# A gate's modulation product moved from TensorE to VectorE in a fused decoder layer

## The reference

```python
sc = jax.nn.silu(c)
mod = sc @ ada_w[l] + ada_b[l]                  # (1024) @ (1024 x 6144)
sh1, sc1, g1, sh2, sc2, g2 = jnp.split(mod, 6)
xn = rmsnorm(x, norm1_g) * (1.0 + sc1) + sh1
proj = xn @ w_in                                # q, k, v, ca, cg
...                                             # 8 heads of causal attention beside
...                                             # a gated convolution of width 31 with group norm
x = x + g1 * (y_mix @ w_out)
xn2 = rmsnorm(x, norm2_g) * (1.0 + sc2) + sh2
h = causal_dwconv(xn2 @ w_up, ffn_dw_w, ffn_dw_b)   # 1024 -> 2 x 2816, width 3
u, g = jnp.split(h, 2, axis=-1)
x = x + g2 * ((silu(g) * u) @ w_down)
```

## Time and profile before

| | |
|---|---|
| runs | 353.32, 354.15, 357.48 us |
| the profiled execution | 354.59 us; from its first to its last instruction (span) 352.8 us |
| mean granted TensorE clock | 0.995 |
| busy, share of the span | TensorE 96%, VectorE 68%, ScalarE 51%, GpSimd 24% |
| moved | 80.05 MB, 227 GB/s over the span |
| chain that ended last | TensorE 88%, DMA 3%, VectorE 3%, ScalarE 2% |

### The profile page before, as it was taken

One profiled execution on the slowest core, in us unless ns is written; L12 is line 12 of the kernel. 1 busy time (PEld: TensorE's weight loads), 2 busy tenths in 40 slices (PEclk: granted clock), 3 DMA queues, 4 the chain that ended last, 5 costly groups with the idle time before them and its releaser, 6 DMA issues.

```text
span 352.8 us, 6291 instructions
## 1 busy us (share of the span) xinstructions
PE 337.0 (96%) x2480; PEld 292.3 (83%) x2480; DVE 239.7 (68%) x467; ACT 178.8 (51%) x266; POOL 85.3 (24%) x134
## 2 busy tenths in 40 slices
PE   7789899999999989999999999999999999999995
PEld 6557788887565468999999999999999989898984
DVE  2654649999964664059886967675858585858556
ACT  4543763444126676547856636373636455454520
POOL 6372099729134086920000000000000000000000
PEclk9989999999999999999999999999999999999999
DMA  7999968989997995330755745554655555400003
GB/s 271 426 424 421 418 255 333 354 307 334 420 352 285 412 378 211 121 119 4 278 200 164 247 185 197 173 207 153 228 154 204 180 180 206 152 0 2 0 2 120
DMA packets 13090, 80.05 MB, mean 227 GB/s; under 512 B 1402, under 2 KB 2818, under 8 KB 3844
## 3 DMA queue, kind: packets, MB, share of 16 engines
q1 hardware_dynamic: 12852, 79.50, 59.5%
q10 hardware_dynamic: 144, 0.13, 0.1%
q0 software_dynamic: 64, 0.01, 0.0%
HBM read 78.57 MB, written 1.06 MB: 226 GB/s over the span
## 4 chain that ended last, share of the span: by engine, by line
PE 88%; DMA 3%; DVE 3%; ACT 2%; issue 2%; SPq 1%; POOL 0%; POOLq 0%; ACTq 0%
PE bank L962 25%; PE bank L964 24%; PE bank L963 24%; PE bank L984 4%; DMA raw<-in_stream 3%; PE bank L1015 2%; ACT w_hi L399 1%; PE bank L1228 1%; DVE prob L813 1%; PE bank L1029 1%; PE bank L1389 1%; PE bank L1345 1%; PE bank L1385 1%; PE bank L1132 1%; PE bank L1386 1%
## 5 line engine op out<-in xcount | busy, mean ns | idle before, releaser
L962 PE MATMUL bank<-act_hi,w_hi 128*128 128x256 f32 x528 | 152.1, 288 | 3.4 <-ACT act_hi L428 1.1
L963 PE MATMUL bank<-act_lo,w_hi 128*128 128x256 f32 x528 | 149.5, 283 | 0.0
L964 PE MATMUL bank<-act_hi,w_lo 128*128 128x256 f32 x528 | 149.5, 283 | 0.0
L962 PEld LDWEIGHTS bank<-act_hi,w_hi 128*128 128x128 f32 x528 | 101.3, 192 | 11.3 <-issue 8.4
L963 PEld LDWEIGHTS bank<-act_lo,w_hi 128*128 128x128 f32 x528 | 101.4, 192 | 0.5
L964 PEld LDWEIGHTS bank<-act_hi,w_lo 128*128 128x128 f32 x528 | 101.4, 192 | 0.0
L399 ACT ACTIVATE w_hi<-raw 128x2048 fp32r<-128x2048 f32 x45 | 85.9, 1908 | 19.7 <-DMA raw<-in_stream 13.7
L637 DVE TENSOR_TENSOR w_lo<-raw,w_hi 128x2048 fp32r<-128x2048 f32 x32 | 73.3, 2292 | 23.2 <-ACT w_hi L399 23.2
L361 POOL TENSOR_TENSOR w_lo<-raw,w_hi 128x256 fp32r<-128x256 f32 (+1 forms) x68 | 63.4, 967 | 38.0 <-ACT w_hi L399 26.5
L722 DVE SCALAR_TENSOR_TENSOR bank<-glu,cols,bank 128x256 f32<-128x256 f32 x116 | 46.0, 480 | 4.2 <-ACT bank L459 4.2
L387 POOL TENSOR_TENSOR xmod<-xr,qk 128x256 f32<-128x256 f32 x1 | 0.7, 722 | 195.7 <-DVE qk L951 195.7
(11 more groups left out here) (186 smaller groups left out, 337.5 us busy)
## 6 DMA issues: line engine op xcount, KB each, us to landing
raw<-in_stream SPq DMA_DIRECT2D x71, 1024.0 KB, 6.3
xt<-in_x_t SPq DMA_DIRECT2D x2, 512.0 KB, 4.6
bias<-toeplitz_rows SPq DMA_DIRECT2D x1, 1024.0 KB, 11.1
xt<-in_x_t SPq DMA_DIRECT2D x1, 1024.0 KB, 8.7
out<-xmod SPq DMA_DIRECT2D x3, 256.0 KB, 2.0
gate<-gate_rows SPq DMA_DIRECT2D x2, 256.0 KB, 6.0
gates_b<-in_ada_b_gates SPq DMA_DIRECT2D x1, 256.0 KB, 8.0
cols<-in_cols SPq DMA_DIRECT2D x1, 185.0 KB, 5.5
```

Of the source, the lines that this page charges most:

```text
L962: nc.tensor.matmul(o, sh, mh, start=first, stop=False)
L963: nc.tensor.matmul(o, sh, ml, start=False, stop=False)
L964: return nc.tensor.matmul(o, sl, mh, start=False, stop=last)
```

## The change

The DRAM image of the weights stays as it is; which halves of its slots are loaded together, and when, changes. Eight slots ("first_half", k) hold g1 and sh2 of row block k, four slots ("scale2", i) hold sc2 of two row blocks, four slots ("gate2", i) hold g2 of two row blocks. Each is loaded by two DMAs of 512 KB. The first twelve stand where the first twelve late ada slots stood; the four places behind them are gone, so the tiles from out 1 on stand four places earlier. The gate2 slots stand ahead of down 2 to down 5.

TensorE takes the twelve slots (`late_row`). g2 is summed by VectorE: eight products of silu(c)'s column with 128x1024 of a slot, added up in `g2_part` (`g2_products`), two behind each of down 1 to down 4. Two matmuls with ones then sum over the partitions ahead of down 6 (`g2_sum`), into bank `UP_BANK[0][0]`; VectorE adds the bias (`g2_rows_out`), and up 16 waits for that. The DMAs of g2's rows go from SP's queue to GpSimd's. g1 and sh2 are turned together, and VectorE reads both (`gate1_shift2_columns`).

```diff
@@ -50,12 +50,35 @@
+def loads():
+
+    late = [("first_half", k) for k in range(KT)] + [("scale2", i) for i in range(KT // 2)]
+    order = []
+    for kind, i in STREAM:
+        if kind == "ada" and i >= KT:
+            if late:
+                order.append(late.pop(0))
+            continue
+        if kind == "down" and 2 <= i < 2 + KT // 2:
+            order.append(("gate2", i - 2))
+        order.append((kind, i))
+    return order
+
+
+LOADS = loads()
+ROWS_USED = {x: n for n, x in enumerate(x for x in LOADS if x[0] in ("ada", "first_half", "scale2"))}
+ARRIVED = {x: 16 * sum(2 if y[0] in HALVES else 1 for y in LOADS[n % RAW:n + 1:RAW]) for x, n in AT.items()}
+G2_SUM_AT = 6
...
-            for n, (kind, i) in enumerate(STREAM):
+            for n, (kind, i) in enumerate(LOADS):
                 if n >= RAW:
-                    k0, i0 = STREAM[n - RAW]
+                    if k0 == "gate2":
+                        sp.wait_ge(g2_step, 2 * i0 + 2)
+                    elif (k0, i0) in ROWS_USED:
+                        sp.wait_ge(ada_used, ROWS_USED[k0, i0] + 1)
                     else:
                         low_made(sp, SP_AT[k0, i0])
-                sp.dma_start(raw[:, n % RAW, :], stream[n]).then_inc(raw_ready[n % RAW], 16)
+                if kind == "first_half":
+                    halves = [(FROM["ada", KT + i], 0), (FROM["ada", 2 * KT + i], 0)]
+                elif kind == "scale2":
+                    halves = [(FROM["ada", 2 * KT + 2 * i + h], 1) for h in range(2)]
+                elif kind == "gate2":
...
+                for to, (row, half) in enumerate(halves):
+                    sp.dma_start(raw[:, n % RAW, to * D_MODEL:(to + 1) * D_MODEL],
+                                 stream[row, :, half * D_MODEL:(half + 1) * D_MODEL]).then_inc(raw_ready[n % RAW], 16)
...
-                if (kind, i) == ("out", 2):
-                    sp.wait_ge(mod_rows_ready, 1)
-                    sp.dma_start(gate_rows, gates_b[64:97:32, :]).then_inc(gates_stored, 16)
...
-                if (kind, i) == ("up", 3):
-                    sp.wait_ge(gates_stored, 16)
-                    sp.wait_ge(qk_ssq, 1)
-                    for n in range(2):
-                        sp.dma_start(gate[:, 0, n * 512:n * 512 + 512], bass.AP(gate_rows.tensor, 512 * n, [[0, P], [1, 512]])
-                                     ).then_inc(gate2_ready, 16)
@@ -382,6 +412,14 @@
+            pool.wait_ge(g2_rows, 1)
+            pool.dma_start(gate_rows, gates_b[64:97:32, :]).then_inc(gates_stored, 16)
+            pool.wait_ge(gates_stored, 16)
+            pool.wait_ge(qk_ssq, 1)
+            for n in range(2):
+                pool.dma_start(gate[:, 0, n * 512:n * 512 + 512], bass.AP(gate_rows.tensor, 512 * n, [[0, P], [1, 512]])
+                               ).then_inc(gate2_ready, 16)
+
...
-            def g1_out():
-
-                act.wait_ge(gates_turned, 1)
-                nc.scalar.activation(g1[:, :].rearrange("p (q j) -> p q j", q=2),
-                                     bank[2][:, :].rearrange("p (j q r) -> p q j r", j=4, q=4)[:, 0:2, :, 0],
-                                     ACT.Copy).then_inc(g1_ready, 1)
+            def sh2_rows_out():
+
+                act.wait_ge(ada_used, 2 * KT)
+                act.wait_ge(glu_ready, CT)
+                nc.scalar.activation(gate_rows1[64:, :], bank[2][64:, :], ACT.Copy).then_inc(sh2_rows, 1)
...
             split_hi(SP_AT["out", 0])
+            sh2_rows_out()
             gn_rows()
...
-                if p == 0:
-                    g1_out()
-                elif p == 1:
+                if p == 1:
                     mod_rows_out()
                     split_hi(SP_AT["out", 1])
                 elif p == 2:
...
+            def gate1_shift2_columns():
+
+                dve.wait_ge(gates_turned, 1)
+                turned_rows = bank[2][:, :].rearrange("p (j q r) -> p q j r", j=4, q=4)
+                nc.vector.tensor_copy(g1[:, :].rearrange("p (q j) -> p q j", q=2), turned_rows[:, 0:2, :, 0]).then_inc(g1_ready, 1)
+                nc.vector.tensor_tensor(shift[:, 1, :].rearrange("p (q j) -> p q j", q=2), turned_rows[:, 2:4, :, 0],
+                                        cols_of("sh2_b").rearrange("p (q j) -> p q j", q=2), ALU.add).then_inc(mod_cols_read, 1)
+
...
+                turned_rows = bank[TURN_BANK][:, :].rearrange("p (j q r) -> p q j r", j=4, q=4)
+                scale2 = scale[:, 1, :].rearrange("p (q j) -> p q j", q=2)
+                nc.vector.tensor_tensor(scale2, turned_rows[:, 0:2, :, 0], cols_of("sc2_b").rearrange("p (q j) -> p q j", q=2),
+                                        ALU.add).then_inc(mod_cols_read, 1)
+                dve.wait_ge(mod_cols_read, 2)
+                nc.vector.tensor_tensor(scale2, turned_rows[:, 2:4, :, 0], scale2, ALU.add).then_inc(mod_cols_read, 1)
+                dve.wait_ge(mod_cols_read, 3)
                 nc.vector.scalar_tensor_tensor(scale[:, 1, :], scale[:, 1, :], 1.0, cols_of("norm2_g"), ALU.add,
                                                ALU.mult).then_inc(mod_cols_read, 1)
-                dve.wait_ge(mod_cols_read, 2)
+                dve.wait_ge(mod_cols_read, 4)
...
+            def g2_products(i):
+
+                arrived(dve, "gate2", i)
+                for h in range(2):
+                    k = 2 * i + h
+                    some = slot("gate2", i)[:, h * D_MODEL:(h + 1) * D_MODEL]
+                    if k == 0:
+                        dve.wait_ge(silu_c_ready, 1)
+                        nc.vector.tensor_scalar(g2_part, some, silu_c[:, k:k + 1], None, ALU.mult).then_inc(g2_step, 1)
+                    else:
+                        dve.wait_ge(g2_step, k)
+                        nc.vector.scalar_tensor_tensor(g2_part, some, silu_c[:, k:k + 1], g2_part, ALU.mult,
+                                                       ALU.add).then_inc(g2_step, 1)
+
+            def g2_rows_out():
+
+                dve.wait_ge(g2_summed, 1)
+                nc.vector.tensor_tensor(gates_b[64:, :], bank[UP_BANK[0][0]][64:, :], gates_b[64:, :], ALU.add).then_inc(g2_rows, 1)
...
-            dve.wait_ge(ada_used, 2 * KT)
-            dve.wait_ge(gates_b_ready, 16)
-            nc.vector.tensor_tensor(gates_b[:, :], bank[2][:, :], gates_b[:, :], ALU.add).then_inc(mod_rows_ready, 1)
+            g1_rows()
...
                 if p == 0:
+                    gate1_shift2_columns()
                     gn_scale()
...
-            norm2_columns()
+            scale2_columns()
@@ -929,7 +998,11 @@
                 done = m > m0 and SPLIT[m - 1][0] == "up"
                 if done:
                     earlier_taps(SPLIT[m - 1][1])
+                if m > m0 and SPLIT[m - 1] == ("down", G2_SUM_AT):
+                    g2_rows_out()
                 split_lo(m + 2)
+                if m > m0 and SPLIT[m - 1][0] == "down" and 1 <= SPLIT[m - 1][1] <= KT // 2:
+                    g2_products(SPLIT[m - 1][1] - 1)
                 if done:
                     gate_hidden(SPLIT[m - 1][1])
                     hid_low(SPLIT[m - 1][1])
...
+            def late_row(kind, i):
+
+                arrived(pe, kind, i)
+                to = bank[2] if kind == "first_half" else bank[7]
+                if (kind, i) == ("scale2", 0):
                     pe.wait_ge(tap, PAIR_TAPS[0])
                 for q in range(4):
-                    last = nc.tensor.matmul(bank[to][32 * q:32 * q + 32, :], silu_c[:, k:k + 1].to_broadcast([P, 32]),
-                                            slot("ada", n)[:, 512 * q:512 * q + 512], start=(k == 0), stop=(k == KT - 1))
+                    k = i if kind == "first_half" else 2 * i + q // 2
+                    last = nc.tensor.matmul(to[32 * q:32 * q + 32, :], silu_c[:, k:k + 1].to_broadcast([P, 32]),
+                                            slot(kind, i)[:, 512 * q:512 * q + 512], start=(i == 0),
+                                            stop=(i == (KT if kind == "first_half" else KT // 2) - 1))
                 last.then_inc(ada_used, 1)
...
             pair_scores(0)
             late_ada(1)
             gn_turn()
-            late_ada(1)
             head_turn(0)
             turn_gates()
             head_turn(1)
@@ -1301,13 +1369,12 @@
             pair_scores(1)
             pe.wait_ge(v_ready, ST)
             pair_values(0)
-            late_ada(2)
             head_turn(2)
-            late_ada(1)
             head_turn(3)
             pair_scores(2)
             pair_values(1)
             pe.wait_ge(g1_ready, 1)
+            pe.wait_ge(mod_cols_read, 1)
             pe.wait_ge(gn_scaled, CT)
...
+                if t == 2 * G2_SUM_AT + 4:
+                    pe.wait_ge(g2_rows, 1)
...
+            def g2_sum():
+
+                pe.wait_ge(g2_step, KT)
+                pe.wait_ge(tap0, 2 * (2 * G2_SUM_AT + 3))
+                for q in range(2):
+                    last = nc.tensor.matmul(bank[UP_BANK[0][0]][64 + 32 * q:96 + 32 * q, :], ones[:, 0:32],
```

(5 more changed lines are left out.)

58 lines of the change are left out of this document (28 added, 30 removed).

## The result

The changed kernel takes 360.58 us, the median of 3 runs (357.26 to 361.80), against 354.15: 1.0154 times the kernel before, 95% interval 1.0096 to 1.0212. A second set of six runs gave 360.88 us and 1.0151 (1.0091 to 1.0211). The forecast was 355.5 us, its range ended at 357.6. The profiled execution took 361.8 us, its span is 360.0 us, its mean granted clock 0.972 (before 0.995).

What follows compares the result with a forecast made beforehand. TensorE was taken as the bound, busy 337.0 of 352.8 us. Profiled 354.59 - 0.4 (removal) + 1.8 (sum's wait) = 356.0, put at 355.5 us because the median lies 0.44 below the profiled run; range 353.2 to 357.6 us.

Steps and rivals of the forecast that it cites:

- Rival (b): Attention stage: with slots removed TensorE's clock falls to half, costing about 1.7 us, ending at 357.1 us; chance 0.20.
- the later places: Removed slots, two behind pair 0's values, one between heads 2 and 3: at most 0.16 and 0.42 us gained, not adding.
- the first place: Removed slot behind the group norm's turning, at 110.48 us: worth 0, since head 0 starts at 112.16 us either way.
- The removal brings 0.4 us: Attention stage: four modulation slots leave TensorE, 3.8 us of work, of which 0.4 us comes off the end.
- The sum and its wait, 1.8 us: Ahead of up 16: TensorE waits for VectorE's bias addition, 1.8 us of delay, two matmuls inside it; ends 0.5 and 2.3.
- the 0.7 that was to show it: Sign near 292 us: a gap of 0.7 to 1.1 us on TensorE ahead of up 16, released by VectorE.
- The second norm: One more VectorE instruction for the second scale, covered by 6.67 us of idle time at 149.79 us: cost 0.
- The products: Among the down tiles: eight VectorE products of 128x1024, 1.22 us each (0.6 to 1.9), cost 0.
- The halved loads: Twelve slots arrive as two DMAs of 512 KB each; conv 3 is the tightest consumer: cost 0.
- (c): Rival: the half-slot loads land late, 1.7 us at conv 3, ending at 357.2 us; chance 0.05.
- (d): Rival: VectorE bounds the down tiles; products of 3.0 us lose 0.7 us in each of four rounds, 358.3 us; chance 0.03.
- The 0.97 for within 2%: Whole kernel: chance 0.97 that the time stays within 2% (7 us); slower 0.02, faster 0.01.

Runs made afterwards that it cites:

- e5: The changed kernel timed once more, nothing altered: 360.88 us, 1.0151 times the kernel before.
- e8: The changed kernel with 17 unused transposes at the start and VectorE's bias addition right behind the taps of up 15: 359.83 us, ratio 1.0117.
- e9: The kernel before with 17 unused transposes at the start, its last four modulation slots cut to one matmul of one column each: 355.04 us, ratio 1.0013.
- e13: The kernel before with 17 unused transposes at the start, its last four modulation slots wholly off TensorE, ring places freed early: 357.68 us, ratio 1.0051.
- e14: e8 with one matmul of one column at each of the four places of the removed slots: 357.99 us, ratio 1.0103.
- e7: The kernel before with 17 unused transposes on TensorE at the start: 354.17 us, ratio 0.9974.
- e11: e8 with an unused stand-in for the removed slot ahead of head 0 only: 359.25 us, ratio 1.0077.
- e10: e8 with three unused stand-ins behind pair 0's values and between heads 2 and 3: 356.53 us, ratio 1.0036.
- e12: e7 with seven more unused transposes around the second norm: 353.65 us, 0.9951 times the kernel before.
- e2: The changed kernel with an unused stand-in for only the removed slot between the group norm's turn and head 0: 357.97 us, ratio 1.0098.
- e3: The changed kernel with three unused stand-ins behind pair 0's values and between heads 2 and 3, none ahead of head 0: 356.73 us, ratio 1.0070.
- e6: The kernel before with three of the four matmuls left out in each of the last four modulation slots: 354.70 us, ratio 0.9996.
- e4: The changed kernel with all four removed slots replaced by unused stand-ins and VectorE's bias addition right behind the taps of up 15: 356.87 us, ratio 1.0075.
- e1: The changed kernel with unused stand-in matmuls at all four places of the removed slots: 359.50 us, ratio 1.0104.

## Why the prediction was wrong

**The clock is the step that failed.** Rival (b) described the mechanism and its place, had a chance of 0.20 and a price of one fall of 3.4 us at half its length, 1.7 us (the sum behind it wrote 1.6). Emptying the places brought a fall in the profiled run and, over e5, e8, e9, e13 and e14, 7.1 us or more at half clock in 42 runs of 42; the kernel before had less than 7 in 21 of 35, and warmed (e7) in 10 of 11, its run of 548.3 us left out. Of the kernels warmed at the start, those with the later places empty (e8, e9, e11, e13, e14) had 13.5 us or more in 29 runs of 48, those with them filled (e7, e10, e12) in none of 35. It cost 51.20 - 46.07 = 5.1 us in the changed kernel's trace, against e2's. Two readings went wrong. First, the evidence against it, that the trace "already has such gaps", looked at one wait of 0.61 us. After the change that wait is 1.61 us, right ahead of where five of the falls begin, and two more follow within 8 us of it, where the matmuls had stood back to back: 1.70 and 0.60 us at full clock (e2), 0.72 and 0.51 us at half (the changed kernel). The prediction costed the first place at nothing, since head 0 starts at the same time with it or without; for the clock it wasn't nothing. The prediction said itself that TensorE would be busy "much less" between pair 0's values and the turn of head 3, and then weighed the average of 14 us against the earlier trace rows. Second, the length of the only fall in the trace was taken as the length of any fall. In this stage it was 17.1, 10.2 or 3.4 us. Half its length was too dear a price, on the other hand: 3.4 us near 22 us cost 1.0 to 1.1 us (the first marker at 108.8 to 108.9 us with that fall, 107.7 to 107.8 in e2 and e3 without), 10.2 us cost 49.88 - 46.07 = 3.8 us (e11), 17.1 us cost 5.1 us. The Trainium skill, TensorE: Matmul & The Clock Gate, section A second HAM failure mode: psum-queue depth-cycling, gave the rule that micro-idles between groups can set the clock swinging; this case's traces agree, at 0.50 for 17.1 us, and should have had more weight.

**The removal brings 0.4 us: right.** e2's trace, at full clock and with the first place filled, has 0.42 us less in stage A. The first place was costed at 0, and e3's trace, at full clock with that place alone empty, has the 46.49 us of the kernel before. That the slots bring 0.42 of 3.8 us was right, that they could be taken out at no cost was not: their work filled TensorE's waits for the softmax chain and held up the clock.

**The sum and its wait, 1.8 us: right in kind, short by 0.2.** Measured 2.0 us (5.19 to 7.20 us). The low part of hidden tile 15 and the addition do stand in front of up 16, and the visible gap is 0.60 us, a little under the 0.7 that was to show it. The two matmuls took 1.05 us, over the prediction's end of 1.0: half of the slot's matmuls isn't half of its time, as e6 shows. The working gave them no price beside the wait; e4 shows what is left with the wait gone, 1.17 us, above the 0.5 of the lower end.

**The second norm: costed at 0, measured 0.35.** In the changed kernel and its variants VectorE's first low part waits 0.61 us for ScalarE, in the kernel before and its variants 0.25 us. The columns are those of the time line of VectorE; the first row is the kernel before's, the second the changed kernel's.

```profile
159.79 0.49 DVE L885 SCALAR_TENSOR_TENSOR act_lo<-xmod,shift,act_hi 128x256 fp32r<-128x256 f32 x1 [0.25 <-ACT act_hi L584]
```
```profile
164.99 0.48 DVE L954 SCALAR_TENSOR_TENSOR act_lo<-xmod,shift,act_hi 128x256 fp32r<-128x256 f32 x1 [0.61 <-ACT act_hi L620]
```

No run isolates why; it stays open. The prediction had set the second scale's added instruction at 0 by VectorE's idle 6.67 us; whether that instruction is the cause isn't shown.

**The rest was right.** The products take 1282 ns (forecast 1220), the first, without an addend, 747; rounds with them last 17.11 us, so they cost 0. The halved loads cost 0: 40.00 of 40 us busy, though the DMA share rose from 0.83 to 0.89; rivals (c) and (d) did not happen. Modulation matmuls on 512 columns have 96 records and the sum 4. Without the clock the forecast would have held: e3's four runs with none at half clock take 355.5 to 355.9 us, though with three places refilled. The 0.97 for within 2% holds by the median (1.5%, interval 1.0 to 2.1%), the range does not.

## What to carry to other kernels

Work that costs nothing because an engine waits there anyway may still be what keeps TensorE's clock up: before taking matmuls out of a stage with short waits, list the gaps that will be left one behind the other, the ones costed at nothing too, and give the fall of the clock a price for several lengths, not for the one in the trace. Put unused transposes at the thin places and time them; here 24 of them made the kernel before 0.5% faster. And read each run's granted clock beside its time, since a median over few runs mixes lengths of the fall.

## What was not expected of the hardware

- One float32 matmul of 128x512 into 32 columns of the array takes 1.04 us, and four side by side 1.06 us (e6).
- The clock fell for 3.4, 6.8, 10.2 or 17.1 us in these traces, with no other length but for falls cut off by the end of the run, and in the five traces with a fall in the attention stage that were warmed at the start (e8, e9, e11, e13, e14) a second one of 3.4 us began 30.7 us after the clock had come back, at 159.5 to 160.4 us.
- At half clock the stages slowed by three to four tenths of the time spent there, not by half: 1.0 to 1.1 of 3.4 us, 3.8 of 10.2, 5.1 of 17.1.
- Unused transposes seem to hold the clock up as matmuls do. With 17 of them at the start none of eight traces (e7 to e14) falls near 22 us, without them five of eight do (before, after, e1, e4, e6). In e7 TensorE is busy 7.66 of 8.00 us from 18 to 26 us:

```profile
18.00:26.00 8.00, 7.66 (x76) 5.85 (x76) 5.08 (x15) 3.78 (x6) 6.30 (x22) 1.00 1.01 421
```
